# The gate bias added by a one-row product on TensorE, the spread gates taken out of PSUM by ScalarE

## What is computed

```python
def _adaln(cond, w, b):
    mod = (jax.nn.silu(cond) @ w + b)[:, None, :]
    return jnp.split(mod, 6, axis=-1)
...
        def sublayers(h, mod, side):
            y = jnp.concatenate([y_a[side], y_b[side], y_c[side], y_d[side]], axis=-1) @ w_out[layer]
            h = _norm(DEEPNORM_ALPHA * h + mod[2] * y, ln_g[layer, 0], ln_b[layer, 0])
            f = _conv_ffn(_modulate(h, mod[3], mod[4]), ...)
            return _norm(DEEPNORM_ALPHA * h + mod[5] * f, ln_g[layer, 1], ln_b[layer, 1])
```

## Time and profile before

| | us |
|---|---|
| median of 3 runs | 1713.68 |
| lowest, highest | 1712.07, 1714.19 |
| profiled execution, its own time | 1715.59 |
| span of its instructions | 1713.8 |

### The profile page before, as it was taken

The page is one execution under the profiler, slowest core; times in us unless marked ns, Lnnn a source line. Parts: engine busy times, 40 slices in busy tenths (PEclk is TensorE's granted clock), DMA queues, the critical chain, the costliest instruction groups (busy, mean ns, idle before and its releaser), DMA issues. The chain is left out here.

```text
span 1713.8 us, 28786 instructions
## 1 busy us (share of the span) xinstructions
PE 1583.7 (92%) x11804; PEld 1253.4 (73%) x11804; DVE 1059.7 (62%) x1812; ACT 645.5 (38%) x1100; POOL 70.0 (4%) x110
## 2 busy tenths in 40 slices
PE   6999999969899999999999979999978898999997
PEld 4766776745688688888888867778754677678885
DVE  2286345897867574554443365734776866578766
ACT  4355222445321263222222253433245321366652
POOL 0000011300100000000000000000010110000000
PEclk8999899989999999999999989999979899899998
DMA  9411111166101143222232032222236101355561
GB/s 389 149 61 38 54 58 49 38 230 240 52 3 52 50 190 130 99 98 99 93 105 74 0 115 74 62 61 75 74 127 244 52 2 52 111 190 190 197 202 44
DMA packets 41330, 180.93 MB, mean 106 GB/s; under 512 B 4720, under 2 KB 5488, under 8 KB 33392
## 3 DMA queue, kind: packets, MB, share of 16 engines
q1 hardware_dynamic: 41200, 179.09, 29.7%
HBM read 178.03 MB, written 1.05 MB: 104 GB/s over the span
## 5 line engine op out<-in xcount | busy, mean ns | idle before, releaser
L236 PE MATMUL ps<-hr_in,wr_in 128*128 128x512 f32 (+1 forms) x544 | 221.9, 408 | 12.4 <-DVE wr_in L229 11.5
L238 PE MATMUL ps<-hr_in,wr_in 128*128 128x512 f32 (+1 forms) x544 | 210.0, 386 | 0.0
L237 PE MATMUL ps<-hr_in,wr_in 128*128 128x512 f32 (+1 forms) x544 | 210.0, 386 | 0.0
L236 PEld LDWEIGHTS ps<-hr_in,wr_in 128*128 128x128 f32 x544 | 109.5, 201 | 62.5 <-issue 36.0
L229 DVE TENSOR_TENSOR wr_in<-mix,wr_in 128x1024 fp32r<-128x1024 f32 x68 | 83.9, 1234 | 88.2 <-ACT wr_in L225 84.8
L236 PE MATMUL ps<-mix_r,work_r 128*128 128x512 f32 (+1 forms) x352 | 133.8, 380 | 1.6 <-DVE work_r L229 1.6
L237 PE MATMUL ps<-work_r 128*128 128x512 f32 (+1 forms) x356 | 135.1, 379 | 0.0
L229 DVE TENSOR_TENSOR work_r<-pr,work_r 128x2048 fp32r<-128x2048 f32 x38 | 86.9, 2288 | 67.7 <-ACT work_r L225 63.6
L238 PE MATMUL ps<-mix_r,work_r 128*128 128x512 f32 x320 | 124.5, 389 | 0.0
L238 PEld LDWEIGHTS ps<-hr_in,wr_in 128*128 128x128 f32 x544 | 109.2, 201 | 19.5
L237 PEld LDWEIGHTS ps<-hr_in,wr_in 128*128 128x128 f32 x544 | 109.5, 201 | 15.6 <-issue 0.2
(11 more groups left out here) (536 smaller groups left out, 3258.5 us busy)
## 6 DMA issues: line engine op xcount, KB each, us to landing
mix<-in_w_in SPq DMA_DIRECT2D x68, 512.0 KB, 3.6
pr<-in_w_up SPq DMA_DIRECT2D x28, 1024.0 KB, 4.9
pr<-in_ada_w SPq DMA_DIRECT2D x40, 512.0 KB, 6.8
ring<-in_w_up SPq DMA_DIRECT2D x16, 1024.0 KB, 4.9
ring<-in_ada_w SPq DMA_DIRECT2D x28, 512.0 KB, 4.5
pr<-in_w_down SPq DMA_DIRECT2D x14, 1024.0 KB, 5.0
pr<-in_ada_w SPq DMA_DIRECT2D x8, 1024.0 KB, 15.8
work<-in_w_out SPq DMA_DIRECT2D x16, 512.0 KB, 3.7
```

Of the source, the lines that this page charges most:

```text
L236: nc.tensor.matmul(out, sh, mh, start=first, stop=False)
L237: nc.tensor.matmul(out, sh, ml, start=False, stop=False)
L238: return nc.tensor.matmul(out, sl, mh, start=False, stop=last)
```

## The change

The bias goes into bank 6 ahead of the copy to `rowb`, so the spread gate has it already. The DMA brings one row of each bias in place of 128. In a gate job PE puts a product `bias` (L1665) ahead of the second and of the fourth quarter, with one contraction row: a row of ones times 256 columns of the bias, into output rows 0 to 31 of bank 6. The instruction L1792 leaves DVE's list. ACT gets `gate_out` (L1983), a copy of bank 7 to the gate, at the places where `row_out` stands and at four late places; `spread_out` of a gate is now signalled by ACT.

```diff
@@ sync
-                        sp.dma_start(gate_of(E, layer, which, sides(layer)[0]), A["gate_b"][layer, which]).then_inc(S("gate_b"), 16)
+                        sp.dma_start(gate_of(E, layer, which, sides(layer)[0])[0:1], A["gate_b"][layer, which]).then_inc(S("gate_b"), 16)
@@ tensor: weights
                     pe.wait_ge(S(f"a{i % SLOTS}"), 16 * (i // SLOTS + 1))
+                    if i % 2 and is_gate(JOBS[q]):
+                        bias(JOBS[q][1], i % 4 // 2)
                     job_blocks(nc, ps[6], cond, slot(i), i % 4 // 2, (i % 2,)).then_inc(S("ada"), 1)
+
+            def bias(n, ch):
+                pe.wait_ge(S("gate_b"), 32)
+                o = (n % 2) * 512 + ch * 256
+                nc.tensor.matmul(ps[6][0:32, ch * 256:(ch + 1) * 256], c(C_ONES, 32, 1),
+                                 gate_of(E, layer, n // 6, sides(layer)[0])[0:1, o:o + 256], start=False, stop=False)
@@ vector: spread_out
-                    dve.wait_ge(S("spread"), u + 1)
                     if side is None:
+                        dve.wait_ge(S("spread"), u + 1)
                         dve.wait_ge(S("mod_b"), 16)
                         coefficients(nc, E, modb, JOBS[q], ps[7][:, 0:8]).then_inc(S("spread_out"), 1)
-                    else:
-                        dve.wait_ge(S("gate_b"), 32)
-                        n = JOBS[q][1]
-                        g, base = (gate_of(E, layer, n // 6, v)[:, (n % 2) * 512:(n % 2 + 1) * 512] for v in (side, sides(layer)[0]))
-                        nc.vector.tensor_tensor(g, base, ps[7][:, :], ALU.add).then_inc(S("spread_out"), 1)
@@ scalar
+            def gate_out(p):
+                if 2 <= p < 2 + len(parts):
+                    q, side = parts[p - 2]
+                    if side is not None:
+                        n = JOBS[q][1]
+                        act.wait_ge(S("spread"), p - 1)
+                        nc.scalar.copy(gate_of(E, layer, n // 6, side)[:, (n % 2) * 512:(n % 2 + 1) * 512], ps[7][:, :]).then_inc(S("spread_out"), 1)
...
                 for p in (*ahead, *behind):
+                    gate_out(p)
                     row_out(p)
...
             low_rank_out(1, 0)
+            gate_out(late[0])
             row_out(late[0])
             low_rank_out(1, 1)
+            gate_out(late[1])
...
             key_exponentials(E, S, act, R, 0, 1)
+            for p in late[2:]:
+                gate_out(p)
             key_exponentials(E, S, act, R, 0, 2)
```

More of the change, by code:

```diff
@@ L3455, in lay_out @@
     mod_b = np.repeat(ada_b.reshape(L, 6, KD, P)[:, [0, 1, 3, 4]].transpose(3, 0, 1, 2), 2, axis=3).reshape(P, L * 8 * KD)
-    gate_b = np.broadcast_to(ada_b.reshape(L, 6, D)[:, 2::3, None, :], (L, 2, P, D))
+    gate_b = ada_b.reshape(L, 6, D)[:, 2::3, None, :]
     ln = np.stack([ln_g, ln_b], axis=2).reshape(L, 2, 1, 2 * D)
```

## The result

| | before | changed kernel |
|---|---|---|
| median of all runs timed together, us | 1712.36 (20 runs) | 1719.76 (20 runs) |
| ratio of the two, 95% interval | | 1.0046 (1.0026 to 1.0065) |
| same, a second series | 1712.77 (29 runs) | 1719.94 (12 runs), 1.0043 (1.0023 to 1.0064) |

The changed kernel is 0.45% slower, 7 to 8 us. The forecast was 1718.4 us and +4.7 us: the sign and the range were right, the size was short by some 3 us. The ratios, and the means further down, leave out two slow runs of the changed kernel, 1730.96 and 3066.70 us.

A forecast was written before the change was run, and what follows sets the result against it. PE was taken to bound the stage, the others mostly waiting for it. Lateness of +2.2 us in layer 0 and +2.5 in layer 1 gave +4.7 on the median of 1713.7, so 1718.4 us; 8 in 10: 1714.0 to 1721.2.

The forecast's parts named there:

- The product's price: PE's gate jobs, both layers: each of sixteen one-row products takes 0.60 us, 9.6 us in all; ends 0.44 and 0.70.
- the lone product: A 256-column product in front of smaller ones at 1464.35 us, keeping PE 0.64 us from its next start, busy 0.70.
- The clock at the first gate job: Layer 0: PE's granted clock is 0.50 at 366 to 369 us; two new products fall there, still priced at 0.60 us.
- DVE's relief: Twelve additions, 7.2 us, leave DVE's list; this pays only in PE's waits, about 3.5 us in layer 0, 1.1 in layer 1.
- The rival that DVE was late: Both layers' rounds: DVE bounds each round, so the time falls to 1706.5 us; chance 0.06 for 1706.5 to 1710.
- The `kT_out` copy: Layer 0, second gate job: ScalarE's copy stands behind the gate copy, and PE's transposes wait 0.6 us more, lateness +2.4.
- Layer 1: -0.7 us from sooner loads, then lateness +1.8 after two gate jobs, +1.3 after the third, +2.5 at the fourth.
- The fourth job's +1.2: Layer 1, last gate job: its two products make PE 1.2 us later, all of it paid, giving +2.5 us.
- The work: The sum of PE's lateness over both layers with 0.60 us for each product: +4.7 us, without a change of clock.
- one spell more in each layer: Clock rival: one more slow spell in each layer costs PE about 1.5 us each, +7.7 in all, 1721.4 us; chance 0.12.
- The sum's rule: Sixteen products, both layers: each 0.1 us of price is 1 us of the sum; +3.1 at 0.44, +5.7 at 0.70.
- Checks promised: Profile after: L1665 16 pairs, next start 0.5 to 0.7 us behind; `rowb` copies at 371.8 and 428.1; stages 95.4 and 71.2 us.

The follow-up runs named there:

- the sibling kernel: The changed kernel with the bias put into row 127 of the row tile by 2 KB DMAs, without products, VectorE copying the gates out: 1716.36 us, ratio 1.0024 to before.

## Why the prediction was right, and where it was short

- **The product's price.** Forecast 0.60 us with 0.44 and 0.70 as ends; measured 0.68 at 2.4 GHz. Its two bounds were well chosen: 0.42 to 0.44 us is what a product in the neighbours' shape takes, and 0.68 is near the lone product. With 0.68 the sum would have been +5.5 us. The rule of the Trainium skill (TensorEngine Tiling (Array Packing), Tiling Modes, Key Properties) that a change of tiling mode drains TensorE fits the other 0.24 to 0.26 us. It spoke against this change rightly, but for the smaller part of the price, and no row shows the drain itself.
- **The clock at the first gate job.** The step took 0.60 us there as everywhere. Three of the sixteen products in this profile ran at 1.2 GHz, the first of them for 1.15 us (above); the earlier trace rows showed that clock, and this could have been in the sum (+1 us).
- **DVE's relief.** Right: the additions and PE's waits for them are gone, and DVE waits instead. ScalarE's copy left PE a wait of 0.7 us at L947, where 0.4 was forecast. At the first gate job DVE's collection starts at 378.17 us behind a wait of 4.52 us for PE's scores, where it had run on at 377.17 us without a wait. The rival that DVE was late (1706.5 us) is out: with the products away the gain is 2.0 us of the 7.2. One argument against it was misread: PE's longest wait for a collection is not 1.0 us but the 3.5 us for L1838. It stands ahead of the first gate job, so DVE's relief can't shorten it, and it was 4.0 us after the change.
- **The `kT_out` copy.** Forecast +0.6 us. In this profile it isn't to be seen: the copy runs at 395.57 us, but the scores ahead of the transposes take until 397.6 at half clock and hide it. In the kernel without products PE does wait 0.7 us there.
- **Layer 1.** Forecast +2.5 us, measured +3.8 by the matched instructions (3.7 by the windows). Ahead of the first gate job PE was 2.9 us early, not 0.7. The four quarters of the job ahead of it landed 2.0 to 2.5 us sooner, counted from the start of the stage, which is within the forecast. PE could use that, and came 1 us further ahead, because it ran this job and the scores behind it at the higher clock. The same sixteen instructions of that job, before at 1.2 GHz, in the change at 2.4:

```profile
1282.64 2.14 PE L447 MATMUL ps<-ring,cond 128*32 128x256 f32 x16
1289.03 1.07 PE L447 MATMUL ps<-ring,cond 128*32 128x256 f32 x16
```

From there to the end of the stage PE lost 6.8 us, where 3.2 were forecast, with a stretch at half clock at 1295 to 1302 us of the change among it. That the sum of both is only 1.3 us off is partly luck. The fourth job's +1.2 was +1.36.
- **What was mis-sized.** The work: +4.7 us forecast, +3.7 by the fit at equal time at half clock. The clock: nothing in the sum, and a chance of 0.12 for one spell more in each layer; about +4 us by the fit. The total lies in the range because the range took that rival in, and part of that is luck. The sum's rule that each 0.1 us of the price is 1 us is too low: the second product of 0.44 us raised the mean span by 8.1 ± 1.5 us, where the rule gives 4.4, and taking all products away gained 9.6 ± 1.3 us, where it gives 6.6 for 0.68 us each.
- **Checks promised.** L1665 has its sixteen pairs, and the next start comes 0.54 or 0.55 us behind its own in twelve of them, 0.98 or 0.99 in three (1.2 GHz) and 0.63 in one. The copy to `rowb` of the first gate job stands at 373.40 us (371.8 forecast) and of the fourth at 432.65 (428.1 forecast). DVE's waits for scores and for L1643 are longer, as said.

Still open is why this kernel has 14 us (± 3) more at half clock. The long stretch at the first gate job came in all four kernels with one-row products ahead of the second and fourth quarters (five profiles: 20, 20, 20, 17 and 17 us), and in none of the seven profiles of kernels without products (10 us in six, 3 us in one). That speaks for the products there. Against it: the kernel with the DMAs of 2 KB has just as much time at half clock (153 ± 3 us) and no product, the one with doubled products has no more than the change (147 ± 3 us), and the kernel with one-row products ahead of the halves has 3 us at that place and 7 us more at 366 us.

## What to carry to other kernels

Before work is moved to an engine, ask who waits for whom: PE was waited for here and DVE waited. Everything in the change but the products (12 additions off DVE, 12 copies onto ScalarE, smaller DMAs) was worth 2.0 ± 1.1 us, while 16 small products on PE cost 10. A product of one row was as dear here as one of 128 rows on the same output rows (0.44 and 0.42 us), and dearer by 0.24 to 0.26 us between products of another shape; its few multiplications say nothing. Where the granted clock sits at half for part of a stage, price what is added there by rows at that clock, and compare kernels over many runs: two profiles of the same kernel differed by 10 us here.

## What the runs showed of the hardware

- A one-row product between quarters of 128 rows costs 0.68 us, one in the quarters' shape 0.42, the second of two equal one-row products 0.44 (2.4 GHz; fp32, 256 columns).
- With a DMA of 2 KB into one partition issued between two loads of 512 KB on the same queue, the second load landed 2.5 to 3.6 us behind the first at three of four places in layer 0, where it was 1.3 to 1.6 without it (in the sibling kernel 2.3 to 3.0 at all four). Single gaps of 2.6 and 3.1 us came without such a DMA too.
- The same kernel ran in 1705 and in 1716 us, by where and how often its clock was at half; over 108 runs a microsecond more at half clock went with 0.32 us more of span.
